# Cache compression beside a recurrent mixer: sharing the copies of one PSUM bank between ScalarE and VectorE, and a new order of the mixer's small work

## What is computed

```python
def compress_rows(rows, pe, w1, w2):      # the cache, gathered page by page
    ch = rows[:, :n_chunks * 16].reshape(B, n_chunks, 16, G, D)
    proj = jnp.einsum('bnsgd,psdh->pbngh', ch, w1)
    h = proj[0, :, 0:n_blk] + bias[0] + proj[1, :, 1:1 + n_blk] + bias[1]
    return jnp.einsum('bngh,hd->bngd', jax.nn.silu(h), w2)

def step(s, xs):                          # the mixer, chunk after chunk
    a = jnp.cumsum(fb, axis=2)
    att = jnp.einsum('bhtk,bhsk,bhtsk->bhts', qb, kb, decay)
    o = att @ vb + (qb * jnp.exp(a)) @ s
    s = jnp.exp(a_end) * s + (kb * jnp.exp(a_end - a)).T @ vb
```

## Time and profile before

| | |
|---|---|
| median of three runs | 2315.44 us |
| the profiled execution's own time | 2317.62 us |
| its span | 2315.8 us |
| PE (matmul) busy | 2102.4 us, 91% |
| PEld (weight load) busy | 1956.6 us, 84% |
| DVE (VectorE) busy | 1417.0 us, 61% |
| ACT (ScalarE) busy | 1114.0 us, 48% |
| POOL (GpSimd) busy | 689.3 us, 30% |
| stage of the change | some 355 to 1098 us of the span |

### The profile page before, as it was taken

How to read it: one execution, slowest core, us unless ns; L and a number is a source line. 1 busy time by engine, 2 the same in 40 slices (tenths; PEclk the granted TensorE clock), 3 DMA queues, 4 the chain that set the end, 5 groups by cost and what they waited for, 6 DMA issues and landing times. The chain is left out here.

```text
span 2315.8 us, 43796 instructions
## 1 busy us (share of the span) xinstructions
PE 2102.4 (91%) x17158; PEld 1956.6 (84%) x17158; DVE 1417.0 (61%) x3026; ACT 1114.0 (48%) x2322; POOL 689.3 (30%) x996
## 2 busy tenths in 40 slices
PE   6999997888888898886688989898999999999998
PEld 5999996787887788775477878686999999999997
DVE  5213225656565664566568778637887878765567
ACT  4115115667766766662447557524333333334334
POOL 0001104545554545431028769312111111110000
PEclk9999998899999999897779989999999999999999
DMA  4215645645455455537911011231223233356352
GB/s 124 65 46 169 233 169 162 196 148 180 151 165 173 149 159 161 170 83 212 300 49 55 6 46 47 73 108 54 88 78 108 94 98 112 89 188 224 107 179 93
DMA packets 226052, 295.70 MB, mean 128 GB/s; under 512 B 23986, under 2 KB 161426, under 8 KB 224658
## 3 DMA queue, kind: packets, MB, share of 16 engines
q1 hardware_dynamic: 199224, 191.65, 26.8%
q0 software_dynamic: 26624, 101.27, 13.4%
HBM read 217.12 MB, written 82.63 MB: 129 GB/s over the span
## 5 line engine op out<-in xcount | busy, mean ns | idle before, releaser
L1568 POOL TENSOR_TENSOR C<-C,a_mt 128x264 f32<-128x264 f32 x66 | 69.3, 1069 | 405.2 <-ACT C L1653 271.0
L3423 PE MATMUL cpt<-ident,X 128*128 128x128 f32 x768 | 124.8, 288 | 69.2 <-ACT a_raw L3137 56.5
L3423 PEld LDWEIGHTS cpt<-ident,X 128*128 128x128 f32 x768 | 95.2, 149 | 90.5 <-ACT a_raw L3137 61.3
L3480 PE MATMUL cplain<-a_XH,w1H 128*128 128x256 f32 x512 | 163.8, 320 | 0.0
L3480 PE MATMUL cplain<-a_XL,w1H 128*128 128x256 f32 x512 | 152.0, 297 | 0.0
L3480 PE MATMUL cplain<-a_XH,w1L 128*128 128x256 f32 x512 | 151.4, 296 | 0.0
L2874 POOL TENSOR_TENSOR a_W<-a_akq 128x64 f32<-128x64 f32 (+1 forms) x232 | 69.4, 299 | 273.2 <-PE chg L3587 189.4
L2087 PE MATMUL f<-a_slot,wd_slot 128*128 128x264 f32 x1176 | 148.3, 285 | 1.8 <-DVE a_slot L1897 1.2
L2050 PE MATMUL f<-a_b,ring 128*128 128x264 f32 x1056 | 143.8, 286 | 4.3 <-DVE a_b L1793 3.7
L2087 PEld LDWEIGHTS f<-a_slot,wd_slot 128*128 128x128 f32 x1176 | 144.8, 188 | 2.7 <-issue 1.8
L2050 PEld LDWEIGHTS f<-a_b,ring 128*128 128x128 f32 x1056 | 135.3, 190 | 4.8 <-issue 4.8
(11 more groups left out here) (617 smaller groups left out, 6593.2 us busy)
## 6 DMA issues: line engine op xcount, KB each, us to landing
v_s<-X SPq DMA_DIRECT2D x64, 256.0 KB, 5.5
a_slot<-a_T SPq DMA_DIRECT2D x20, 792.0 KB, 4.6
raw<-in_w_in POOLq DMA_DIRECT2D x12, 1024.0 KB, 6.0
V<-v_s SPq DMA_DIRECT2D x6, 2048.0 KB, 10.0
raw<-in_w_gate SPq DMA_DIRECT2D x22, 512.0 KB, 5.2
raw_odd<-in_w_val SPq DMA_DIRECT2D x22, 512.0 KB, 5.7
a_T<-C SPq DMA_DIRECT2D x20, 528.0 KB, 3.5
a_T<-sums SPq DMA_DIRECT2D x11, 792.0 KB, 4.5
```

Source lines behind the costliest of these rows:

```text
L1568: nc.gpsimd.tensor_tensor(C[j][:, at], C[j][:, at], mt[:, q % 2, m, c], ALU.mult).then_inc(multiplied, 1)
L3423: last = nc.tensor.transpose(pt[:, c:c + P], X[:, at % SLOTS, h, a, P * kind:P * kind + P], ident[:])
L3480: last = nc.tensor.matmul(out[:, h], w, x, start=(begins and q + h + part == 0), stop=(ends and q + h == 2 and part == 2), skip_group_chec ...
```

## The change

**The turn bank's copies are shared.** `raw_copy` (ScalarE) now copies only group 0, that is `parts[0:2]`; a new `upper_copy` on VectorE copies group 1. Whoever read `raws[k]` or reused the bank after `raw_ready` now waits for both (`raw_whole`).

**Both engines do the k = 0 copies first in each step.** The mixer's work moves: on ScalarE `keep_scores`, `keep_taps`, the exponentials (now in odd steps) and `hidden(u, 1)` (now in the next unit's first step) stand between the two halves; `squares` goes to the end of the next even step, `hidden(u, 0)` to the end of the next unit's first step. On VectorE `results` and the second part of `weigh` (three levels of six products, and the two wide ones) stand in even steps between the k = 0 copies and `low_part` k = 0, `pairs` there in odd steps; the first part of `weigh` (four levels, eight products) stays at the end of the odd step.

**`pairs` reduces once.** One reduction of 128x192 writes `diag` (128x32) in place of four; ScalarE then copies the four 32x32 blocks to the diagonal of `attT` (`diagonals`, at the end of the odd step). TensorE's `outputs` waits for them too (`diag_kept`).

**TensorE** does `wide_products` and the first small products of a chunk after `turn(at+1, 2)` in place of before `project_second(at, 0)`, and the next small ones after `project_second(at, 1)`. GpSimd's `scaled` and SP's output and chunk DMAs move to odd steps.

```diff
+        def raw_whole(eng, at, k):
+            eng.wait_ge(raw_ready[k], at + 1)
+            eng.wait_ge(upper_ready[k], at + 1)
...
             elif kind and at < PAIRS:
-                eng.wait_ge(raw_ready[kind - 1], at + 1)
+                raw_whole(eng, at, kind - 1)
...
+            def diagonals(n):
+                if decode(n):
+                    return
+                act.wait_ge(a_kept, n + 1)
+                for b in range(4):
+                    x = slice(32 * b, 32 * b + 32)
+                    last = nc.scalar.copy(attT[x, n % 2, x], diag[x, :])
+                last.then_inc(diag_kept, 1)
...
-                for g, a in parts:
+                for g, a in parts[0:2]:
                     last = nc.scalar.copy(part_of(raws[k], at, g, a), split(at, g, a))
                 last.then_inc(raw_ready[k], 1)
...
              for at in range(LAST):
                 u, s = at // NS, at % NS
+                first_half(at + 1)
+                if u >= 1 and s == 0:
+                    hidden(u - 1, 1)
                 if at % 2 == 0 and 2 <= at <= PAIRS:
                     keep_scores(at // 2 - 1)
...
+                if s == NS - 1 and u < DB:
+                    keep_taps(u)
+                if at % 2 == 1 and at // 2 + 1 < NN:
                     exponentials(at // 2 + 1)
+                second_half(at + 1)
+                if u >= 1 and s == 0:
+                    hidden(u - 1, 0)
                 if at % 2 == 1:
-                    squares(at // 2)
+                    diagonals(at // 2)
+                elif at >= 2:
+                    squares(at // 2 - 1)
...
-                for b in range(4):
-                    r = slice(32 * b, 32 * b + 32)
-                    last = nc.vector.tensor_reduce(t[r, r], prod[r].rearrange("p l t -> p t l"), AX.X, ALU.add)
-                last.then_inc(a_kept, 1)
+                if n >= 1:
+                    dve.wait_ge(diag_kept, states(n - 1))
+                nc.vector.tensor_reduce(diag[:], prod[:].rearrange("p l t -> p t l"), AX.X, ALU.add).then_inc(a_kept, 1)
...
+            def upper_copy(at, k):
+                if at >= PAIRS:
+                    return
+                dve.wait_ge(t_ready[k], at + 1)
+                if at >= 1:
+                    dve.wait_ge(l_ready[k], at)
+                for g, a in parts[2:4]:
+                    last = nc.vector.tensor_copy(part_of(raws[k], at, g, a), split(at, g, a))
+                last.then_inc(upper_ready[k], 1)
...
+                if at + 1 < LAST:
+                    upper_copy(at + 1, 0)
+                if at % 2 == 0:
+                    if n >= 1 and not decode(n - 1):
+                        results(n - 1)
+                    weigh(n, 1)
+                elif not decode(n):
+                    pairs(n)
                 if at + 1 < LAST:
                     low_part(at + 1, 0)
...
                 if s == NS - 1 and u < DB:
                     join_taps(u)
                 if at + 1 < LAST:
+                    upper_copy(at + 1, 1)
                     low_part(at + 1, 1)
...
                 pe.wait_ge(a_kept, n + 1)
+                pe.wait_ge(diag_kept, states(n))
...
-                if chunk and n >= 1:
-                    wide_products(n)
-                    small_products(n, (0, 1))
                 project_second(at, 0)
                 score(at)
                 turn(at + 1, 2)
                 if chunk and n >= 1:
+                    wide_products(n)
+                    small_products(n, (0, 1))
+                project_second(at, 1)
+                if chunk and n >= 1:
                     small_products(n, (2, 3))
-                project_second(at, 1)
```

More of the change, by code:

```diff
@@ L2767, in compress_and_scan @@
         attT = sb("attT", [P, 2, P])
+        diag = sb("diag", [P, 32])
         attTd = sb("attTd", [DT, DT])
@@ L2790, in compress_and_scan @@
         low0_ready, sum_ready, sumH_ready = (sem(n) for n in ("low0_ready", "sum_ready", "sumH_ready"))
-        raw_ready = [sem("raw_ready0"), sem("raw_ready1")]
+        raw_ready, upper_ready = ([sem(f"{n}{k}") for k in range(2)] for n in ("raw_ready", "upper_ready"))
+        diag_kept = sem("diag_kept")
         h_ready, l_ready, mm_ready = ([sem(f"{n}{k}") for k in range(2)] for n in ("h_ready", "l_ready", "mm_ready"))
@@ L2914, in _ @@
                 if at % 2 == 0:
-                    if at >= 2:
-                        scaled(at // 2 - 1)
                     if 2 <= at <= PAIRS:
                         add_scores(at // 2 - 1)
-                elif (at + 3) // 2 < NN:
-                    differences((at + 3) // 2)
+                    continue
+                if at >= 2:
+                    scaled(at // 2 - 1)
+                if at // 2 + 2 < NN:
+                    differences(at // 2 + 2)
             scaled(NN - 1)
@@ L3043, in _ @@
                     blocks_out(u - 1)
-                if at % 2 == 0 and at >= 2:
+                if at % 2 == 0 and 2 <= at <= PAIRS:
+                    scores(at // 2 - 1)
+                if at % 2 == 1 and at >= 2:
                     n = at // 2 - 1
@@ L3162, in keys_high, with first_half @@
                 nc.scalar.copy(KTH[:], pt[:]).then_inc(kh_ready, 1)
-            def high_parts(at, between=None):
+            def first_half(at):
                 if at < PAIRS:
@@ L3168, in high_parts, with second_half @@
                     high_part(at, 0)
-                if between:
-                    between()
+            def second_half(at):
                 if at < PAIRS:
@@ L3192, in _ @@
                 u, s = at // NS, at % NS
+                first_half(at + 1)
+                if u >= 1 and s == 0:
+                    hidden(u - 1, 1)
                 if at % 2 == 0 and 2 <= at <= PAIRS:
                     keep_scores(at // 2 - 1)
[L3195 to L3202, removed]
+                if s == NS - 1 and u < DB:
+                    keep_taps(u)
+                if at % 2 == 1 and at // 2 + 1 < NN:
                     exponentials(at // 2 + 1)
+                second_half(at + 1)
+                if u >= 1 and s == 0:
+                    hidden(u - 1, 0)
                 if at % 2 == 1:
-                    squares(at // 2)
+                    diagonals(at // 2)
+                elif at >= 2:
+                    squares(at // 2 - 1)
+            for k in range(2):
+                prompt_hidden_rows(k)
+            squares(NN - 1)
             for k in range(2):
@@ L3212, in _, with weigh @@
             flat = lambda x, s: x[:, s].rearrange("p k q h -> p (k q h)")
-            def weigh(n):
+            def weigh(n, part):
                 r = unit(n)[2]
                 k, q = akq[:, n % 4, 2, 0:r], akq[:, n % 4, 1, 0:r]
-                dve.wait_ge(exp_ready, n + 1)
-                for l, half in levels(n):
+                if part == 0:
+                    dve.wait_ge(exp_ready, n + 1)
+                for l, half in levels(n)[4 * part:4 + 4 * part]:
                     w = halves(W[:, n % 2, l, 0:r], half)
@@ L3343, in _ @@
             dve.wait_ge(q_ready, 1)
+            upper_copy(0, 1)
             low_part(0, 1)
@@ L3361, in _ @@
             nc.vector.tensor_copy(bias[:], hg[:, 0:8].rearrange("p (c x) -> p c x", x=2)[:, :, 0]).then_inc(bias_kept, 1)
-            weigh(0)
+            weigh(0, 0)
             dve.wait_ge(hc_in, 64)
@@ L3379, in _ @@
                     queries(u + 1)
-                if at % 2 == 0:
+                if at % 2 == 0 and decode(n):
                     pairs(n)
@@ L3385, in _ @@
                             block_maxima(1, slice(16 * i, 16 * i + 16))
[L3386 to L3399, removed]
+                    results(n)
+                elif decode(n):
+                    for half in range(2):
+                        if at == LAST - 1:
+                            block_maxima(half, slice(32, 48))
+                        decoded(n, half)
+                if at % 2 == 1 and n + 1 < NN:
+                    weigh(n + 1, 0)
                 if at == LAST - 3:
```

8 lines of the change are left out of this document (5 added, 3 removed).

## The result

The changed kernel takes 2293.96 us, the median of five runs (2291.66 to 2301.39), against 2316.19 before (2311.35 to 2321.26): a ratio of 0.9908, 95% interval 0.9883 to 0.9934. It is faster by 22 us, 0.9%, where 47 were forecast. The profiled execution took 2298.45 us, 19.2 less than the one before.

What follows compares the result with a forecast made beforehand. PE waited in even steps for ScalarE's late turn-bank copies, held by order. The 64 steps fall from 657.7 to 612 (-46), the prompt's unit -8, clock +7: -47, giving 2268 us; own range 2252 to 2284, with rivals 2235 to 2303.

Steps and rivals of the forecast that it cites:

- `low_part` k = 0: VectorE's work in even steps after `weigh` and before its k = 1 copies: taken as 1.1 us, ending at 4.5.
- `blocks` at 1.4: Extra work at s = 4 of each unit: said to add 1.4 us, giving a step of 10.8 us.
- the clock: PE's clock falling at long waits (s = 7, s = 0): some five falls, 7 us charged against the change.
- decode pairs: Step pairs with decode work, in three units: 21.0 us forecast against 22.74 before, 3.85 above other pairs.
- the hole: PE's wait in even steps for ScalarE's late turn-bank copies, held by the order of small work; forecast to go.
- turn 2 is late next: Even steps: PE wants turn 2 at 4.93 us and gets it at 5.4, after VectorE's k = 1 copies.
- the rival on that: ScalarE and VectorE take turns reading the bank: 1.6 us a copy pair, 2356 us in all; 4%.
- `join_taps` now holds the copies: At s = 7 its 2.7 us lies before VectorE's k = 1 copies: turn 2 at 7.95, step 10.9 us.
- s = 0: First step of a unit: table load and two activations delay `project_second` to 4.7, turn 2 to 6.7; step 10.3 us.
- s = 1: Second step of a unit: the table load back to Exp; forecast 8.55 us.
- the 0.14 that `XL` lost beside GpSimd: VectorE's `XL` at 0.83 against 0.69 us; by the contention rule 0.14 each odd step, 4 us on the sum.
- VectorE is late: Rival: each step's turn 2 waits for VectorE, half a microsecond more a step, 2296 us; 20%.

## Why the prediction was wrong

The mechanism was right and the size was not: -22 in place of -47. The steps that failed are terms of the sum: `low_part` k = 0 at 1.1 us in even steps, `blocks` at 1.4, and the clock and the steps behind decode pairs.

**Right.** That the hole is an order and not a cost: the earlier trace rows's wait for `squares` is gone, and turn 1 comes 2.59 us after turn 0 in every plain step. That turn 2 is late next, for VectorE's copies. That two readers of one bank do not take turns: the pair costs 0.87 on VectorE and 0.74 on ScalarE while both read, and the rival on that falls. What the Trainium skill's page "PSUM — Partial Sum Buffer", section "PSUM bank collisions raise a hardware error", says of different quadrants agrees. That `join_taps` now holds the copies: turn 2 at s = 7 5.4 us after turn 1 (5.36 by the working). Outside the decode pairs s = 0 is 10.2 to 10.65 (10.3), and s = 1 is 8.62 in most units (8.55).

**Wrong, first: "`low_part` k = 0, 1.1" in the even step.** It took 2.1, since the sum took 1.39. The change itself brings this about: `keep_scores` moves behind the k = 0 half on ScalarE, and VectorE's sum moves behind `weigh`, and so GpSimd's addition of the kept scores falls on the sum. In the kernel before they never met. The prediction had considered only the 0.14 that `XL` lost beside GpSimd, called it 4 us, and left it out of the sum. In the kernel before GpSimd's differences beside that `XL` (654.95, rows 9) were these:

```profile
654.94 0.29 POOL L2874 TENSOR_TENSOR a_W<-a_akq 128x64 f32<-128x64 f32 x1
655.19 0.74 POOL L2875 TENSOR_TENSOR a_W<-a_akq 128x64 f32<-128x64 f32 x1
```

The numbers fit a wait for what is left of the other engine's running instruction, on either side. `XL` started 0.28 before the end of a difference and lost 0.14; the sum started 1.11 before the end of the addition and lost 0.97; the difference at 655.19, which started 0.59 before the end of `XL`, took 0.74 in place of 0.29; the addition, which started 0.54 before the end of `XL`, took 1.68 in place of 1.28. Each lost some 0.14 less than what was left. Behind eight short additions the sum lost next to nothing (0.43). The rule of the Trainium skill ("SBUF — State Buffer", "Who interferes with whom": a VectorE instruction with two SBUF inputs contends with a GpSimd instruction that reads SBUF) agrees with these rows. Turn 2 came 1.0 later than worked out, and the part behind it was 0.3 shorter (3.32, not 3.64). The plain even steps were 0.6 to 0.7 above their sum at s = 6 and 0.2 to 0.5 at s = 2, and 1.6 in the one where the clock fell: 8 us.

**Wrong, second: "`blocks` adds 1.4".** It was the difference of two steps of the kernel before, in both of which PE waited anyway. Worked out like the other steps, s = 4 would have had 2.59 and the 2.9 of `blocks` and its wait of 0.7 in front of turn 1, 6.2 us, with 2.34 and the prediction's own 3.64 behind: some 12.2. Measured are 6.28, 2.36 and 3.28, together 11.92 in place of 10.8, and seven of them are 8 us. Leaving out 1.84 us of its matmuls made the step 1.64 shorter.

**Wrong, third: the clock, and the steps after decode pairs.** Behind the waits of 2.2 to 3.0 us at s = 7 the clock fell in five of the first seven units: 10.8 to 13.1 us against 10.9, 8 us over the sum, about the 7 that had been charged for all falls together. It fell in the steps after the decode pairs too (at = 18, 36 and 54: 10.85, 13.61 and 10.87 us), which the prediction had not worked out:

```profile
557.43:568.28 10.85, 10.62 (x112) 9.75 (x112) 8.90 (x29) 4.85 (x12) 4.09 (x5) 0.78 0.30 83
738.87:752.48 13.61, 12.71 (x136) 11.38 (x136) 9.65 (x30) 4.95 (x12) 4.06 (x5) 0.87 0.42 122
```

Turn 1 did not wait for a copy there. PE came to it late, because its matmuls ran at half clock for part of the step: in `project_first` of at = 18 they lie 0.21 us apart, at full clock 0.12. They are 5 us over. In two of the three places (at = 36 and 54) the clock fell in the kernel before as well. Odd steps were 0.17 over, some 3 us in all. 8 + 8 + 8 + 5 + 3 = 32 is what lies between 643.8 and 612; 7 of it was charged, 25 are missing. Two more terms cancel: the decode pairs themselves were 3 us over, and the very last step, which has no copies for `join_taps` to hold, took 7.7 and not 10.9.

Of the rivals, "VectorE is late" came nearest: 2296 was its number, and the measured 2294 lies on it. That is in part luck: it had half a microsecond more in each of the 64 steps for VectorE, and of the 32 us over only some 11, the plain even and the odd steps, are of that kind; the rest is `blocks` and the clock. I gave it 20% and the forecast 52%, because I had no single instruction that could be late; which GpSimd instruction would run beside each moved VectorE instruction was the question left out.

What stays open: why the clock falls in one unit and not in the next at nearly equal waits (s = 7 11.06 in unit 1, 12.77 in unit 2; both waited 2.9 to 3.0 us before turn 2).

## What to carry to other kernels

When small work is reordered, list for each moved instruction what now runs beside it, above all a GpSimd instruction beside a VectorE one with two SBUF inputs, and take what can be left of the neighbour's instruction as the price; here cutting the long one in pieces took the price away. Do not take the cost of a block of work from the difference between two steps that wait for other things: lay its busy time and its own wait into the working of the new step. And a queue that takes over urgent copies needs every long item in front of them moved: sharing alone was 2% slower, with the order and the single reduction 1% faster, and with the last long items out of the way 2.5%.

## What was unexpected of the hardware

A VectorE addition of 128x256 with both inputs in SBUF, 0.42 us alone, took 1.39 us when it started inside a GpSimd addition of 64x512, and ended 0.3 us after it; GpSimd's addition was longer too, 1.68 against 1.28, where it had started inside a VectorE instruction with two SBUF inputs. Cut into eight of 64x64, GpSimd's took 2.84 us, and VectorE's 0.43. ScalarE and VectorE read disjoint partitions of one PSUM bank at the same time, at 0.37 and 0.43 us a copy of 64x256, ScalarE's exactly as when it read alone (0.366 in either kernel).
